# GLA chunks in pairs with five state buffers, the last activation chunk written into the ring, and norms ahead of low parts in the first FFN step

## The chip, the core and the metric

One core of a Trainium2 chip runs the whole program; the metric is the device time of that core in microseconds. TensorE (PE) multiplies into eight PSUM banks of 2 KB per partition, VectorE (DVE), ScalarE (ACT) and GpSimd (POOL) do the elementwise work, and the queues of SyncE (SP), ACT and POOL start the transfers between DRAM and SBUF.

## The reference

One decoder layer in float32 over 512 prompt tokens and 8 x 4 decode tokens, D = 2048:

```python
h = rmsnorm(x, g_mix) * (1 + sc1) + sh1
z = h @ w_in                      # attention, pooling and gated linear attention (GLA) columns
# GLA, per head: chunks of 32 tokens, state S of 128 x 256
def step(S, xs):
    qd_i, kdec_i, v_i, bl_i = xs
    o_i = qd_i @ S                              # what earlier chunks give
    S = exp(bl_i) * S + kdec_i.T @ v_i          # the state after this chunk
    return S, o_i
x = x + g1 * (mix @ w_out)
h2 = rmsnorm(x, g_ffn) * (1 + sc2) + sh2
gate, up = split(h2 @ w_gu)                     # DFF = 5632
x = x + g2 * ((silu(gate) * up) @ w_down)
y = rmsnorm(x, g_final)
```

## The kernel before, in words

Activations lie transposed, 128 features by 544 tokens a tile, in two halves of 272. Every large product is made of three float32r matmuls: high part of the weight by high and by low part of the activation, and low by high. ACT makes the high part of a weight tile (`hi`, `hi_op`), DVE the low part (`lo`, `lo_op`); both run a fixed list of steps, in program order, and so do PE and the queues. Semaphores are the only order between engines.

**GLA.** Each of 4 heads has six projections (gq, gk, gv0, gv1, gg0, gg1). `project` goes over 16 k; after each k it has 6 matmuls (L1887) behind it and runs whatever side jobs are listed for that k. In gg0 from k = 5 and on into gg1 up to k = 4 the side job is one chunk a k: `chunk(c)` multiplies the chunk's keys by its values (L2113, 32 rows of the array, into PSUM bank 2 or 3), for every fourth chunk the masked inner part of a block of 128 tokens (L2116), and then, once the state before this chunk is there, query by state (L2120, 32 columns of the array) into the chunk's 32 partitions of the block's output. Those are plain float32 products, two instructions each in the trace. DVE's `update(c)` (L1424 and L1429) makes the next state from the bank; there are two state buffers, so that states and queries follow each other chunk by chunk. From k = 6 of gg1 on come the eight decode sequences (L2133, L2140). `spread` and `beside` write the lists.

**FFN.** 44 steps make 128 activation features each (gate and up), then 3 x 8 steps multiply by w_down. The first two steps are plain (`plain_product`, eight products of 24 matmuls); from step 2 on a step is seven products (`product`, L2242) over quarters and their combinations, 24 matmuls each, or 18 where a down step spans three chunks. Weights come two steps ahead (`load_group`, SP). An activation chunk is four steps; after steps 4c+3 and 4c+4 (FT = 44 is the first down step) `turn_parts` on DVE and `parts_hi` on ACT make seven quarters with high and low parts in SQ, from where SP (`store_parts`) stores them to DRAM, twice 952 KB. The down steps read a ring of four chunks in HS; POOL fills it from DRAM (`load_parts`, 544 KB for a quarter of a chunk), the first three chunks as the last gate step, FT - 1, sets the place of each quarter free, the fourth right behind them. PE waits for a quarter in `product`. The saved residual comes back by `load_x1` on the same queue.

**Between them.** `last_two` makes the last two tiles of the output projection, first half of the tokens for both tiles, then the second half. `sum_half(w)` adds up the squares for the norm of one half. Then each (half, row half) goes through `norm` (DVE), `affine` (ACT, and POOL for decode columns), `hs_hi` (ACT) and `hs_lo` (DVE), and `plain_product(0, j)` waits for `hs_lo` at j = 0, 2, 4, 6.

Of the kernel before, what the change touches and what calls it, by code (L numbers as in the profile page):

```python
# [32 lines left out]
P = 128  # L33
# [13 lines left out]
GG0_CHUNKS = 11  # L47
# [164 lines left out]

def nth(s, i=0):

    return OPS * (s - PLAIN) + i


def rows_of(s):

    if s < FT:  # L220
        return [V_FFN + V_CHUNK * (s // FC) + 4 * (s % FC) + j for j in range(4)]
    return [V_FFN + V_CHUNK * (v % NFC) + 4 * FC + (s - FT) % DOWN for v in range(*chunks(s))]
# [12 lines left out]
def program(nc, ctx, ins, outs):  # L235
# [98 lines left out]
    SS = [sb(f"SS{i}", [P, DV]) for i in range(2)]  # L334
    SD = sb("SD", [P, DEC_B, DV])
# [48 lines left out]
    TT = sb("TT", [P, 4, HT])  # L384
    SQ = sb("SQ", [P, 2, 7, HT], F32R)
# [40 lines left out]
    def o_block(b):  # L426

        return PS[:, b // 2, DV * (b % 2):DV * (b % 2) + DV]

# [97 lines left out]
    def af_tile(f):  # L527
        return AF[min(f % 4, 2)]
# [7 lines left out]
    def _(sp):  # L536
# [82 lines left out]
    def _(g):  # L619
# [109 lines left out]
        for h in range(GH):  # L729
            if h:  # L730
                g.dma_start(HP[:, :], ins["head_params"][h]).then_inc(S["head_in"], 16)
            g.dma_start(SD[:, :, :], ins["gla_state"][h]).then_inc(S["state_in"], 16)
            g.wait_ge(S["state_up"], NCH * (h + 1))
            g.wait_ge(S["seq_up"], DEC_B * (h + 1))
            g.dma_start(outs["gla_prompt"][h], SS[0][:, :]).then_inc(S["s_out"], 16)
# [79 lines left out]
    def _(a):  # L815
# [290 lines left out]
        def parts_hi(p, n):  # L1106

            if n == 0:
# [3 lines left out]
                a.activation(SQ[:, 0, 0, :], AF[p % 2][:, 0:HT], ACT.Copy).then_inc(S["af_hi"], 1)  # L1112
            elif n == 1:
                a.activation(SQ[:, 0, 1:3, :], halves(AF[2][:, :]), ACT.Copy).then_inc(S["af_hi"], 1)
            else:
                a.wait_ge(S["t_made"], 4 * p + 4)
                a.activation(SQ[:, 0, 3:7, :], TT[:, :, :], ACT.Copy).then_inc(S["af_hi"], 1)
# [61 lines left out]
        rms(1)  # L1179
# [16 lines left out]
        for s in range(PLAIN, STEPS):  # L1196
            u = s - (STEPS - DOWN)
            for i in range(7):
                if s == PLAIN and i == 1:
                    a.wait_ge(S["hs_lo"], 16)  # L1200
                    a.wait_ge(S["taken"], 2)
                    a.activation(AF[0][:, :], AFX[:, :], ACT.Copy)
                if s == PLAIN and i == 2:
                    plain_gates(1, SG[0][:, :], SG[1][:, :])
                slot(s, i)
                if 3 <= s <= FT and s % 4 in (0, 3):
                    p = 2 * ((s - 3) // 4) + (s - 3) % 4
                    if i == 2:
                        parts_hi(p, 0)
                        parts_hi(p, 1)  # L1210
                    elif i == 3:
                        parts_hi(p, 2)
                if (u, i) in SQUARED:
                    square_x1(SQUARED[u, i])
# [13 lines left out]
    def _(d):  # L1228
# [187 lines left out]
        for h in range(GH):  # L1416
# [3 lines left out]
            def update(c):  # L1420
                last = pcol(c, CH) + CH - 1
                d.wait_ge(S["chunk_mm"], NCH * h + c + 1)
                if c == 0:
                    d.tensor_copy(SS[1][:, :], PS[:, 2, 0:DV]).then_inc(S["state_up"], 1)  # L1424
                    return
                if c == 1:
                    d.wait_ge(S["head_in"], 16 * (h + 1))
                d.wait_ge(S["state_up"], NCH * h + c)
                d.scalar_tensor_tensor(out=SS[(c + 1) % 2][:, :], in0=SS[c % 2][:, :], scalar=EB[:, last:last + 1],  # L1429
                                       in1=PS[:, 2 + c % 2, 0:DV], op0=ALU.mult, op1=ALU.add)\  # L1430
# [84 lines left out]
            for c in range(GG0_CHUNKS, NCH):  # L1515
                update(c)
# [134 lines left out]
        def slot(s, i):  # L1651
# [18 lines left out]
            elif i == 6:  # L1670
# [6 lines left out]
                if s < FT:  # L1677
                    d.wait_ge(S["gate_b"], s + 1)
                    d.tensor_tensor(af_tile(s)[:, HT:NT], SG[1][:, :], W5[:, :], ALU.mult).then_inc(S["taken"], 1)
# [9 lines left out]
        def turn_parts(p, n):  # L1689

            b11, b12 = (AF[p % 2][:, HT * a:HT * a + HT] for a in range(2))
            b21, b22 = (AF[2][:, HT * a:HT * a + HT] for a in range(2))
# [10 lines left out]
            elif n == 2:  # L1703
                for x, src, lo_q, up_q in ((1, AF[p % 2][:, 0:HT].unsqueeze(1), 0, 1), (2, halves(AF[2][:, :]), 1, 3)):
                    d.wait_ge(S["af_hi"], 3 * p + x)
                    d.tensor_tensor(SQ[:, 1, lo_q:up_q, :], src, SQ[:, 0, lo_q:up_q, :].bitcast(F32), ALU.subtract)\
                        .then_inc(S["af_lo"], 1)
            else:
                d.wait_ge(S["af_hi"], 3 * p + 3)
                d.tensor_tensor(SQ[:, 1, 3:7, :], TT[:, :, :], SQ[:, 0, 3:7, :].bitcast(F32), ALU.subtract)\  # L1710
                    .then_inc(S["af_lo"], 1)

# [78 lines left out]
        for s in range(PLAIN, STEPS):  # L1791
            for i in range(7):
# [4 lines left out]
                if 3 <= s <= FT and s % 4 in (0, 3) and 1 <= i <= 4:  # L1797
                    turn_parts(2 * ((s - 3) // 4) + (s - 3) % 4, i - 1)
# [15 lines left out]
    def _(e):  # L1814
# [238 lines left out]
        for h in range(GH):  # L2053
# [50 lines left out]
            def chunk(c):  # L2104
                b, rows = c // 4, slice(CH * (c % 4), CH * (c % 4) + CH)
                if c == 0:
                    e.wait_ge(S["gv_by_token"], 4 * h + 4)
                    e.wait_ge(S["a_masked"], 2 * h + 2)
                elif c == 1:
                    pass  # L2110
                else:
                    e.wait_ge(S["state_up"], NCH * h + c - 1)
                e.matmul(PS[:, 2 + c % 2, 0:DV], KDT[rows, b, :], GVT[rows, b, :], start=True, stop=True)\  # L2113
                    .then_inc(S["chunk_mm"], 1)
                if c % 4 == 0:
                    e.matmul(o_block(b), ATT[:, b, :], GVT[:, b, :], start=True, stop=False, skip_group_check=True)  # L2116
                if c:
                    e.wait_ge(S["state_up"], NCH * h + c)
                    at = pcol(c, CH)
                    mm = e.matmul(o_block(b)[rows, :], GQ[:, at:at + CH], SS[c % 2][:, :],  # L2120
                                  start=False, stop=True, skip_group_check=True)
                if c == NCH - 1:
# [32 lines left out]
            beside("gg0", 4, 10, {3: [lambda: v_turn(1)]}, spread(5, chunk, range(GG0_CHUNKS)))  # L2155
            beside("gg1", 5, 10, spread(0, chunk, range(GG0_CHUNKS, NCH)), spread(6, sequence, range(DEC_B)))

# [13 lines left out]
        def last_two():  # L2171
# [4 lines left out]
            for w in range(2):  # L2176
                for t in range(2):
                    for k in range(KT):
# [3 lines left out]
                        if w == 1 and t == 0 and k == 8:  # L2182
# [12 lines left out]
        def plain_product(s, j):  # L2195
# [6 lines left out]
            for k in range(KT // 2):  # L2202
                if s == 0 and j == 1 and k == 4:
# [15 lines left out]
        def product(s, i):  # L2219
# [13 lines left out]
            if s == FT or s > FT and last > chunks(s - 1)[1]:  # L2233
                e.wait_ge(quarter_in[i], 16 * last)
# [210 lines left out]
```

## Time and profile before

| | us |
|---|---|
| median of 3 runs (2534.06 to 2538.4) | 2534.31 |
| the profiled execution | 2530.13 |
| its span, first to last instruction | 2528.3 |
| PE busy | 2400.5 |
| DVE busy | 1549.9 |
| ACT busy | 921.5 |
| transfers, mean over the span | 170 GB/s |

The first three lines are times of the whole program; the others are within the span. Busy time of PE is not time at its peak: matmuls overlap, and an array that drains between two of them is still counted busy.

### The profile page before, as it was taken

The page shows a single profiled execution, that of the slowest core. Times are in us where ns is not written, and L with a number is a line of the kernel's source. Part 1 is how long each engine was busy: PE and PEld are TensorE (multiplying, and loading weights), DVE is VectorE, ACT ScalarE, POOL GpSimd, SP SyncE. Part 2 cuts the span into 40 slices and gives each one's busy share as a digit, 9 for nine tenths or more (in the row PEclk, how much of TensorE's full clock was granted, in tenths as well). Part 3 has the DMA queues.
Part 4 walks back from the last instruction along what each step waited for, and adds up shares of the span by engine and source line. Part 5 has one row for each costly group of instructions (what it writes and reads, how often), then busy time and mean ns, then how long its engine had stood idle before and what let it go on. Part 6 is the DMA issues. An engine that isn't in the chain of part 4 may idle for free.

```text
span 2528.3 us, 44152 instructions
## 1 busy us (share of the span) xinstructions
PE 2400.5 (95%) x18537; PEld 2198.0 (87%) x18537; DVE 1549.9 (61%) x2234; ACT 921.5 (36%) x1322; POOL 238.0 (9%) x292
## 2 busy tenths in 40 slices
PE   5689999999999899989999999999999979999996
PEld 1189887777777599989999999999999979999996
DVE  0332642323223322379888888888888868888898
ACT  2132431313122312354444444444444433433343
POOL 3150230000000011100000000000000121011131
PEclk9889999999999999999999999999999989999998
DMA  9954464545454243223344334433443596366452
GB/s 343 338 181 160 151 185 137 188 150 188 149 174 157 73 156 107 101 101 123 131 168 164 122 131 170 162 122 131 169 162 124 205 399 249 126 226 216 161 209 96
DMA packets 195606, 430.21 MB, mean 170 GB/s; under 512 B 14740, under 2 KB 120516, under 8 KB 193360
## 3 DMA queue, kind: packets, MB, share of 16 engines
q1 hardware_dynamic: 174720, 345.25, 39.8%
q0 software_dynamic: 18096, 77.68, 8.7%
q10 hardware_dynamic: 2592, 4.46, 0.5%
q8 instruction: 147, 2.41, 0.4%
q14 instruction: 51, 0.42, 0.0%
HBM read 369.35 MB, written 57.98 MB: 169 GB/s over the span
## 4 chain that ended last, share of the span: by engine, by line
PE 89%; DMA 4%; DVE 3%; issue 1%; ACT 1%; SPq 0%; POOL 0%; DVEq 0%; ACTq 0%; POOLq 0%
PE PJ L2242 26%; PE PS L2242 26%; PE PJ L1887 24%; DMA AR<-in_weights 3%; PE PJ L1840 2%; PE PS L2113 2%; PE PS L2120 1%; DMA GR<-in_weights 1%; PE PJ L1830 1%; PE PJ L2209 1%; PE PS L2140 1%; PE PS L2133 1%; PE PJ L1852 1%; PE PJ L2186 1%; ACT X L1127 1%
## 5 line engine op out<-in xcount | busy, mean ns | idle before, releaser
L2242 PE MATMUL PS<-HS,WO 128*128 128x272 f32 x5376 | 683.5, 289 | 15.8 <-DVE W L1616 13.7
L2242 PEld LDWEIGHTS PS<-HS,WO 128*128 128x128 f32 x5376 | 679.0, 188 | 16.9 <-DVE W L1616 13.9
L2242 PE MATMUL PJ<-HS,WO 128*128 128x272 f32 x5376 | 681.1, 288 | 0.4 <-DVE WO L1593 0.3
L2242 PEld LDWEIGHTS PJ<-HS,WO 128*128 128x128 f32 x5376 | 677.3, 188 | 0.9 <-issue 0.9
L1081 ACT ACTIVATE WO<-GR 128x1024 fp32r<-128x1024 f32 (+1 forms) x462 | 477.0, 1033 | 495.2 <-PE PJ L2242 233.6
L1593 DVE TENSOR_TENSOR WO<-GR,WO 128x1024 fp32r<-128x1024 f32 (+1 forms) x462 | 556.1, 1204 | 134.4 <-ACT WO L1081 134.3
L1887 PE MATMUL PJ<-HH,WH 128*128 128x272 f32 x1568 | 350.8, 305 | 20.7 <-issue 7.9
L1887 PE MATMUL PJ<-HH,WL 128*128 128x272 f32 x1568 | 327.8, 291 | 0.0
L1887 PE MATMUL PJ<-HL,WH 128*128 128x272 f32 x1568 | 327.7, 291 | 0.0
L1887 PEld LDWEIGHTS PJ<-HH,WH 128*128 128x128 f32 x1568 | 248.0, 192 | 72.4 <-issue 61.3
L1232 DVE TENSOR_TENSOR WL<-RW,WH 128x1024 fp32r<-128x1024 f32 x102 | 128.5, 1264 | 289.7 <-ACT WH L820 289.4
L1887 PEld LDWEIGHTS PJ<-HL,WH 128*128 128x128 f32 x1568 | 250.4, 192 | 0.0
L1887 PEld LDWEIGHTS PJ<-HH,WL 128*128 128x128 f32 x1568 | 249.2, 192 | 0.0
L820 ACT ACTIVATE WH<-RW 128x1024 fp32r<-128x1024 f32 x102 | 107.3, 1054 | 187.1 <-PE PJ L1887 187.1
L1830 PE MATMUL PJ<-AR,CS 128*32 128x512 f32 x256 | 68.7, 685 | 50.4 <-DMA AR<-in_weights 50.2
L775 POOL DMA_DIRECT2D HS<-act_parts x98 | 69.8, 713 | 331.3 <-PE PJ L2242 204.8
L1830 PEld LDWEIGHTS PJ<-AR,CS 128*32 128x32 f32 x256 | 9.8, 115 | 103.2 <-DMA AR<-in_weights 87.5
L1429 DVE SCALAR_TENSOR_TENSOR SS<-SS,EB,PS 128x256 f32<-128x256 f32 x60 | 28.8, 480 | 95.9 <-PE PS L2113 95.9
L780 POOL DMA_DIRECT2D X<-x_kept x4 | 2.3, 566 | 900.2 <-PE PJ L2242 881.2
L1609 DVE TENSOR_TENSOR GR<-GR 128x1024 f32<-128x1024 f32 (+1 forms) x66 | 78.7, 1193 | 6.9
L1616 DVE TENSOR_TENSOR W<-W,PJ 128x272 f32<-128x272 f32 x132 | 57.4, 435 | 36.2 <-PE PJ L2242 35.9
L1601 DVE TENSOR_TENSOR GR<-GR 128x1024 f32<-128x1024 f32 (+1 forms) x66 | 78.3, 1186 | 1.2 <-DMA GR<-in_weights 1.2
(303 smaller groups left out, 1930.5 us busy)
## 6 DMA issues: line engine op xcount, KB each, us to landing
GR<-in_weights SPq DMA_DIRECT2D x264, 512.0 KB, 6.8
AR<-in_weights SPq DMA_DIRECT2D x256, 256.0 KB, 4.6
HS<-act_parts POOLq DMA_DIRECT2D x98, 544.0 KB, 7.0
RW<-in_weights SPq DMA_DIRECT2D x102, 512.0 KB, 4.5
act_parts<-SQ SPq DMA_DIRECT2D x44, 952.0 KB, 7.4
AR<-in_weights SPq DMA_DIRECT2D x64, 512.0 KB, 5.2
MIX<-in_xT SPq DMA_DIRECT2D x1, 4352.0 KB, 16.5
X<-in_xT POOLq DMA_DIRECT2D x4, 1088.0 KB, 9.7
```

What stands on the lines that cost most here:

```text
L775: g.dma_start(HS[:, HS_AT[QUARTER[i]], :, at:at + 2, :].bitcast(F32), XQ[QUARTER[i], :, :, c:c + 2, :])\
L820: a.activation(WH[v.mod(HIS)][:, :], RW[v.mod(RAW)][:, :], ACT.Copy).then_inc(S["hi"], 1)
L1081: a.activation(split_part(n, 0), operand(n), ACT.Copy).then_inc(S["w_hi"], 1)
L1232: d.tensor_tensor(WL[v.mod(RAW)][:, 0:n], RW[v.mod(RAW)][:, 0:n], WH[v.mod(HIS)][:, 0:n].bitcast(F32), ALU.subtract).then_inc(S["lo"], 1)
L1593: d.tensor_tensor(split_part(n, 1), operand(n), split_part(n, 0).bitcast(F32), ALU.subtract)\
L1601: d.tensor_tensor(a21, a21, a22, ALU.add).then_inc(S["combined"], 1)
L1609: d.tensor_tensor(a12, a12, a11, ALU.subtract).then_inc(S["combined"], 1)
L1616: d.tensor_tensor(out[:, :], dst[:, :], src, ALU.add).then_inc(S["sums"], 1)
L1830: mm = e.matmul(PJ[j:j + CP, 2 * pair, :], CS[:, k, :], AR[n % AS][:, 512 * c:512 * c + 512], start=(k < 4), stop=(k >= KT - 4))
L1840: mm = e.matmul(PJ[CP * x:CP * x + CP, 2 * pair, 0:HB], CS[:, 4 * s + x, :], AR[n % AS][:, HB * x:HB * x + HB], start=(s == 0), stop=(s == ...
L1887: mm = e.matmul(out[w], x, y[:, k, HT * w:HT * w + HT], start=(k == 0 and n == 0), stop=(k == KT - 1 and n == 2))
L2242: mm = e.matmul(out, w[part], HS[:, HS_AT[QUARTER[i]], y, (2 * first + k) % (KT // 2), :], start=OPENS[i] and k == 0 and x == 0, stop=k == ...
```

## The change

GLA: five state buffers. `pair_up(n)` issues the key-by-value products of chunks 2n and 2n+1 one behind the other, every second k, and `block_out(b)` the three or four query-by-state products of a block together, two steps later. The other state buffers lie where GB and GT are dead. FFN: the two half chunks of the last activation chunk (p = 20 and 21) are not stored and loaded, but written by ACT and DVE straight into the ring's fourth place, during steps FT and FT+1; the order of chunks in the ring becomes 0, 1, 2, 10, 3, ... First FFN step: on DVE and ACT `norm`, `half_residual`, `reciprocal`, `affine` and `rms` change places with `hs_lo` and `plain_lo`, and PE has `sum_half` earlier.

```diff
+RING = (0, 1, 2, NFC - 1) + tuple(range(3, NFC - 1))
+    TURNED.update({(ss, n + 1): (pp, n) for n in range(4)})
+    PARTED.update({(ss, 2): (pp, (0, 1)), (ss, 3): (pp, (2,))})
+TURNED.update({(FT - 1, 1): (KEPT, 0), (FT - 1, 2): (KEPT, 1), (FT, 1): (KEPT, 2), (FT, 2): (KEPT, 3)})
+TURNED.update({(FT, 3): (KEPT + 1, 0), (FT, 4): (KEPT + 1, 1), (FT + 1, 1): (KEPT + 1, 2), (FT + 1, 2): (KEPT + 1, 3)})
+for pp in range(2):
+    PARTED.update({(FT + pp, 0): (KEPT + pp, (0, 1)), (FT + pp, 1): (KEPT + pp, (2,))})
...
-            if 3 <= s <= FT and s % 4 in (0, 3):
+            if 3 <= s <= FT - 4 and s % 4 in (0, 3):
                 store_parts((s - 3) // 4, (s - 3) % 4)
...
-            if i == 5:
-                g.wait_ge(S["af_lo"], 3 * (2 * NFC - 1))
-                load_x1(1)
-        for i in range(OPS):
-            load_parts(FT - 1, i, 3)
-        g.wait_ge(S["parts_out"], 64 * NFC)
+        g.wait_ge(S["af_lo"], parts_made(KEPT, 4))
+        load_x1(1)
+        for v in range(4, 11):
             for i in range(OPS):
                 load_parts(last_use(v - 4), i, v)
+                if v == 4 and i == 4:
+                    g.wait_ge(S["af_lo"], parts_made(KEPT + 1, 4))
+                    load_x1(2)
+            if v == 4:
+                load_x1(3)
...
+                if p >= KEPT:
+                    a.wait_ge(S["w_used"], nth(FT))
+                    a.activation(HS[:, HS_AT[0], 0, at, :], x[:, 0:HT], ACT.Copy).then_inc(S["af_hi"], 1)
+                    return
...
         affine(0)
         hs_hi(0)
         half_x1(KT - 2, 1)
+        half_x1(KT - 1, 1)
         affine(1)
-        half_x1(KT - 1, 1)
+        rms(1)
         plain_hi(0, 2)
         plain_hi(0, 3)
         hs_hi(1)
-        rms(1)
...
-            for c in range(GG0_CHUNKS):
-                if c == 6:
+            for c in range(12):
+                if c == 4:
                     lo(v + (1 + LEAD))
-                if c == 7:
+                if c == 8:
                     head_mod("gg0")
                 update(c)
...
         norm(0)
+        d.wait_ge(S["x1_out_a"], 32)
+        norm(1)
         half_residual(KT - 2, 1)
         hs_lo(0)
-        d.wait_ge(S["x1_out_a"], 32)
-        norm(1)
         half_residual(KT - 1, 1)
+        reciprocal(1)
         plain_lo(0, 2)
         plain_lo(0, 3)
+        norm(2)
         hs_lo(1)
-        reciprocal(1)
-        norm(2)
-        hs_lo(2)
         d.wait_ge(S["x1_out_b"], 32)
         norm(3)
+        hs_lo(2)
...
+            def pair_up(n):
+                b = n // 2
+                if n == 0:
...
+                else:
+                    e.wait_ge(S["state_up"], NCH * h + 2 * n)
+                for c in (2 * n, 2 * n + 1):
+                    rows = slice(CH * (c % 4), CH * (c % 4) + CH)
+                    e.matmul(chunk_up(c), KDT[rows, b, :], GVT[rows, b, :], start=True, stop=True)\
+                        .then_inc(S["chunk_mm"], 1)
+                if n % 2 == 0:
+                    e.matmul(o_block(b), ATT[:, b, :], GVT[:, b, :], start=True, stop=False, skip_group_check=True)
...
+            def block_out(b):
+                e.wait_ge(S["state_up"], NCH * h + 4 * b + 3)
+                for j in range(4):
+                    c, rows = 4 * b + j, slice(CH * j, CH * j + CH)
+                    if c:
+                        at = pcol(c, CH)
+                        mm = e.matmul(o_block(b)[rows, :], GQ[:, at:at + CH], SS[c % STATES][:, :],
+                                      start=False, stop=True, skip_group_check=True)
...
+                return {k: [lambda: block_out(n // 2 - 1)] + jobs if n and n % 2 == 0 else jobs}
+            beside("gg0", 4, 10, {3: [lambda: v_turn(1)]}, *[chunks_of(5 + 2 * n, n) for n in range(6)])
+            beside("gg1", 5, 10, chunks_of(1, 6), chunks_of(3, 7), {5: [lambda: block_out(NB - 1)]},
+                   spread(6, sequence, range(DEC_B)))
...
-                        if w == 1 and t == 0 and k == 8:
+                        if w == 1 and t == 0 and k == 4:
                             sum_half(0)
...
-                if s == 0 and j == 1 and k == 4:
+                if s == 0 and j == 0 and k == 4:
                     sum_half(1)
...
-                e.wait_ge(quarter_in[i], 16 * last)
+                e.wait_ge(quarter_in[i], 16 * (last - (last > 3)))
+            if s > FT and last == 4 and i == 0:
+                e.wait_ge(S["af_lo"], parts_made(KEPT + 1, 4))
```

## Rows read from the trace of the kernel before

**Rows 1.** The page, chain that ended last: share of the span by engine.

```profile
PE 89%; DMA 4%; DVE 3%; issue 1%; ACT 1%; SPq 0%; POOL 0%; DVEq 0%; ACTq 0%; POOLq 0%
```

**Rows 2.** Chain of work on PE, GLA chunks of head 0: start us, us, what.

```profile
405.15 0.62 PE PS L2113 x2
405.77 0.63 PE PS L2116 x2
406.40 0.76 PE PJ L1887 x6
...
407.78 0.55 PE PS L2120 x2
408.33 0.95 PE PJ L1887 x6
...
440.36 0.95 PE PJ L1887 x6
```

**Rows 3.** The same view, two other lines that use part of the array.

```profile
272.75 1.16 PE PS L1997 x16
...
441.31 1.86 PE PJ L1840 x32
```

**Rows 4.** Timeline of DVE, a state update: start, us, line, operation, [idle <-releaser].

```profile
407.82 0.48 DVE L1429 SCALAR_TENSOR_TENSOR SS<-SS,EB,PS 128x256 f32<-128x256 f32 x1 [1.59 <-PE PS L2113]
```

**Rows 5.** The page, costliest groups: low part of a weight tile, mean ns.

```profile
L1232 DVE TENSOR_TENSOR WL<-RW,WH 128x1024 fp32r<-128x1024 f32 x102 | 128.5, 1264 | 289.7 <-ACT WH L820 289.4
```

**Rows 6.** Timeline of PE, steps FT and FT+1.

```profile
2023.99 9.20 PE L2242 MATMUL PS<-HS,WO 128*128 128x272 f32 x72
2034.41 2.49 PE L2242 MATMUL PS<-HS,WO 128*128 128x272 f32 x18 [1.22 <-issue]
2050.56 6.18 PE L2242 MATMUL PS<-HS,WO 128*128 128x272 f32 x36 [13.66 <-DVE W L1616]
...
2073.41 15.96 PE L2242 MATMUL PS<-HS,WO 128*128 128x272 f32 x126
```

**Rows 7.** Waits, 1990 to 2130 us: who, for whom, us, times, longest.

```profile
ACT SQ L1112 <- DMA act_parts<-SQ: 16.6, 1, 16.6
```

**Rows 8.** Timeline of POOL: loads of the ring's fourth place, held by the third's landing.

```profile
2034.61 0.72 POOL L775 DMA_DIRECT2D HS<-act_parts x1 [3.73 <-DMA HS<-act_parts]
...
2045.84 0.72 POOL L775 DMA_DIRECT2D HS<-act_parts x1 [5.12 <-DMA HS<-act_parts]
```

**Rows 9.** Timeline of SP's queue: stores of the last two half chunks.

```profile
2018.75 1.04 SPq L598 DMA_DIRECT2D act_parts<-SQ  x2
...
2052.61 0.98 SPq L598 DMA_DIRECT2D act_parts<-SQ  x2
```

**Rows 10.** Windows: us, busy of PE PEld DVE ACT POOL, clock, DMA share, GB/s.

```profile
2040.00:2045.00 5.00, 0.00 (x0) 0.00 (x0) 0.00 (x0) 0.00 (x0) 0.71 (x1) 0.50 1.03 414
...
2075.00:2080.00 5.00, 5.00 (x42) 5.00 (x41) 4.90 (x8) 2.38 (x4) 0.39 (x1) 1.00 1.03 414
```

**Rows 11.** Timeline of DVE: low parts of an activation's turned quarters.

```profile
2051.29 1.29 DVE L1710 TENSOR_TENSOR SQ<-TT,SQ 128x1088 fp32r<-128x1088 f32 x1
```

**Rows 12.** Timeline of PE, the first FFN step (j = 0, j = 4) and the second's start.

```profile
1074.46 3.27 PE L2209 MATMUL PS<-HS,WO 128*128 128x272 f32 x24 [1.33 <-DVE HS L1729]
...
1096.41 5.48 PE L2209 MATMUL PS<-HS,WO 128*128 128x272 f32 x24 [4.34 <-DVE HS L1729]
...
1112.44 3.19 PE L2209 MATMUL PJ<-HS,WO 128*128 128x272 f32 x24
```

**Rows 13.** Timeline of DVE there: reciprocal and norm.

```profile
1086.78 1.85 DVE L1723 RECIPROCAL RN<-RN 128x272 f32<-128x272 f32 x1
1088.66 2.50 DVE L1718 TENSOR_TENSOR X<-X,RN 128x1088 f32<-128x1088 f32 x2
```

**Rows 14.** Timeline of ACT there: affine, high parts.

```profile
1067.94 4.05 ACT L1127 ACTIVATE X<-X,MOD 128x256 f32<-128x256 f32 x8 [3.31 <-DVE X L1718]
...
1093.94 2.09 ACT L1139 ACTIVATE HS<-X 128x1088 fp32r<-128x1088 f32 x2
```

More of the change, by code:

```diff
@@ L46 @@
 NCH = SEQ // CH
-GG0_CHUNKS = 11
+STATES = 5
 TAU = 16.0
@@ L210, with parts_made @@
 SQUARED.update({(u, i): 2 * u - (i == 2) for u in range(4, DOWN) for i in (2, 6)})
+KEPT = 2 * NFC - 2
+RING = (0, 1, 2, NFC - 1) + tuple(range(3, NFC - 1))
+TURNED, PARTED = {}, {}
+for pp in range(KEPT):
+    ss = 4 * (pp // 2) + 3 + pp % 2
+    TURNED.update({(ss, n + 1): (pp, n) for n in range(4)})
[4 more added lines that the diff above has]
+    PARTED.update({(FT + pp, 0): (KEPT + pp, (0, 1)), (FT + pp, 1): (KEPT + pp, (2,))})
+def parts_made(p, n):
+    return 3 * p + max(p - KEPT, 0) + n
 def nth(s, i=0):
@@ L221, in rows_of @@
         return [V_FFN + V_CHUNK * (s // FC) + 4 * (s % FC) + j for j in range(4)]
-    return [V_FFN + V_CHUNK * (v % NFC) + 4 * FC + (s - FT) % DOWN for v in range(*chunks(s))]
+    return [V_FFN + V_CHUNK * (v % NFC) + 4 * FC + (s - FT) % DOWN for v in map(lambda v: RING[v % NFC], range(*chunks(s)))]
 def groups_in(s):
@@ L334, in program @@
     SS = [sb(f"SS{i}", [P, DV]) for i in range(2)]
+    SS += [sb(f"SS{i + 2}", [P, DV], at=gb_at + 4 * DV * i) for i in range(STATES - 2)]
     SD = sb("SD", [P, DEC_B, DV])
@@ L428, in o_block, with chunk_up @@
         return PS[:, b // 2, DV * (b % 2):DV * (b % 2) + DV]
+    def chunk_up(c):
+        return PS[:, 2 + c % 2, 0:DV]
     def bank_decode(ps):
@@ L527, in af_tile @@
     def af_tile(f):
-        return AF[min(f % 4, 2)]
+        return AF[3 if f == FT - 1 else min(f % 4, 2)]
     block = ctx.enter_context(nc.Block())
@@ L1106, in parts_hi @@
         def parts_hi(p, n):
+            x, up = AF[p % 2], AF[3 if p > KEPT else 2]
+            at = KT // 2 - 2 + p % 2
             if n == 0:
                 a.wait_ge(S["taken"], 2 * (4 * (p // 2) + p % 2 + 3))
+                if p >= KEPT:
+                    a.wait_ge(S["w_used"], nth(FT))
+                    a.activation(HS[:, HS_AT[0], 0, at, :], x[:, 0:HT], ACT.Copy).then_inc(S["af_hi"], 1)
+                    return
                 if p:
                     a.wait_ge(S["parts_out"], 32 * p)
-                a.activation(SQ[:, 0, 0, :], AF[p % 2][:, 0:HT], ACT.Copy).then_inc(S["af_hi"], 1)
+                a.activation(SQ[:, 0, 0, :], x[:, 0:HT], ACT.Copy).then_inc(S["af_hi"], 1)
             elif n == 1:
-                a.activation(SQ[:, 0, 1:3, :], halves(AF[2][:, :]), ACT.Copy).then_inc(S["af_hi"], 1)
+                out = HS[:, HS_AT[1]:HS_AT[1] + 2, 0, at, :] if p >= KEPT else SQ[:, 0, 1:3, :]
+                a.activation(out, halves(up[:, :]), ACT.Copy).then_inc(S["af_hi"], 1)
             else:
                 a.wait_ge(S["t_made"], 4 * p + 4)
-                a.activation(SQ[:, 0, 3:7, :], TT[:, :, :], ACT.Copy).then_inc(S["af_hi"], 1)
+                if p < KEPT:
+                    a.activation(SQ[:, 0, 3:7, :], TT[:, :, :], ACT.Copy).then_inc(S["af_hi"], 1)
+                    return
+                for y in (0, 2):
+                    q = HS_AT[3 + y]
+                    a.activation(HS[:, q:q + 2, 0, at, :], TT[:, y:y + 2, :], ACT.Copy).then_inc(S["af_hi"], 1)
         def affine(b):
@@ L1205, in _ @@
                 slot(s, i)
[L1206 to L1212, printed above, removed]
+                if (s, i) in PARTED:
+                    for n in PARTED[s, i][1]:
+                        parts_hi(PARTED[s, i][0], n)
                 if (u, i) in SQUARED:
@@ L1514, in _ @@
             lo(v + LEAD)
-            for c in range(GG0_CHUNKS, NCH):
+            for c in range(12, NCH):
                 update(c)
@@ L1691, in turn_parts @@
             b11, b12 = (AF[p % 2][:, HT * a:HT * a + HT] for a in range(2))
-            b21, b22 = (AF[2][:, HT * a:HT * a + HT] for a in range(2))
+            up, at = AF[3 if p > KEPT else 2], KT // 2 - 2 + p % 2
+            b21, b22 = (up[:, HT * a:HT * a + HT] for a in range(2))
             t1, t2, t3, t4 = (TT[:, x, :] for x in range(4))
@@ L1703, in turn_parts @@
             elif n == 2:
[L1704 to L1708, printed above, removed]
+                for x, src, lo_q, up_q in ((1, AF[p % 2][:, 0:HT].unsqueeze(1), 0, 1), (2, halves(up[:, :]), 1, 3)):
+                    q = HS_AT[lo_q]
+                    hi, lo = (HS[:, q:q + up_q - lo_q, part, at, :] if p >= KEPT else SQ[:, part, lo_q:up_q, :]
+                              for part in range(2))
+                    d.wait_ge(S["af_hi"], parts_made(p, x))
+                    d.tensor_tensor(lo, src, hi.bitcast(F32), ALU.subtract).then_inc(S["af_lo"], 1)
+            elif p < KEPT:
                 d.wait_ge(S["af_hi"], 3 * p + 3)
@@ L2154, in _, with chunks_of @@
             beside("gv1", 6, 11, {4: [lambda: v_turn(0)]})
-            beside("gg0", 4, 10, {3: [lambda: v_turn(1)]}, spread(5, chunk, range(GG0_CHUNKS)))
-            beside("gg1", 5, 10, spread(0, chunk, range(GG0_CHUNKS, NCH)), spread(6, sequence, range(DEC_B)))
+            def chunks_of(k, n):
+                jobs = [lambda: pair_up(n)]
+                return {k: [lambda: block_out(n // 2 - 1)] + jobs if n and n % 2 == 0 else jobs}
+            beside("gg0", 4, 10, {3: [lambda: v_turn(1)]}, *[chunks_of(5 + 2 * n, n) for n in range(6)])
+            beside("gg1", 5, 10, chunks_of(1, 6), chunks_of(3, 7), {5: [lambda: block_out(NB - 1)]},
+                   spread(6, sequence, range(DEC_B)))
         project_two(At(M_OUT), At(T_OUT), KT, A_FIRST + N_HB, {4: [lambda: o_turn(GH - 1)]})
@@ L2232, in product @@
             first, last = chunks(s)
-            if s == FT or s > FT and last > chunks(s - 1)[1]:
-                e.wait_ge(quarter_in[i], 16 * last)
+            if s == FT or s > FT and last > chunks(s - 1)[1] and last > 4:
+                e.wait_ge(quarter_in[i], 16 * (last - (last > 3)))
+            if s > FT and last == 4 and i == 0:
+                e.wait_ge(S["af_lo"], parts_made(KEPT + 1, 4))
             n, tiles = nth(s, i), 2 * slots(s)
```

51 lines of the change are left out of this document (19 added, 32 removed).

## The prediction

> **What bounds the kernel now.** I read the page first. The chain that ended last is PE for 89% of the span [rows 1], so a change pays by what it takes off PE: products, drains of the array, waits. Then I read the chain of work on PE and the timelines of the three places that the diff touches.
>
> *GLA chunks.* Six projection matmuls (L1887) take 0.76 us when they follow a full-array product and 0.95 us when they follow a chunk's query product [rows 2]. So leaving a part-array product for the full array costs 0.19 us. A chunk adds 0.62 (L2113) and 0.55 (L2120), and every fourth 0.63 more (L2116). There is no wait on a semaphore that matters here: PE is the bound, with work that fills little of the array. From the first chunk (405.15) to the matmuls behind the last (440.36) are 35.21 us; 15 groups at 0.76 and 0.4 for turning modulation rows leave 23.4. From below: 16 x 0.62 + 4 x 0.63 + 15 x 0.55 = 20.7, and 14 returns to the full array at 0.19 = 2.7, together 23.4. The other three heads repeat the pattern.
>
> *First down steps.* 126 matmuls take 15.8 us (the last row of [rows 6] shows 15.96 with the end of the last one). FT starts at 2023.99, FT+2 at 2073.41, where 31.6 us would do: 17.8 us are lost. PE stands 13.66 us for a sum on DVE. DVE was behind ACT, and ACT waited 16.6 us for a store of SQ [rows 7] which was issued at 2018.75 [rows 9], when the transfers were saturated: about 414 GB/s at a DMA share of 1.03 [rows 10]. In the same stretch PE's clock fell to 0.50 of full, its lower level of 1.2 GHz. Quarters 4 and 6 of the first three ring chunks had landed at 2034.6 and 2045.8, since the fourth chunk's loads wait for that [rows 8].
>
> *First FFN step.* Its eight products of 24 matmuls and one sum (1.25 us) would take 25.4 us without waits. They begin at 1074.46, 1.33 us late, and the second step begins at 1112.44 [rows 12]: 39.3 from 1073.1, so 14 us are lost. The longest wait, 4.34 us, brought the lower clock: 24 matmuls in 5.48 instead of 3.2. All these waits end with `hs_lo` or with the squares of the second half.
>
> **Part 1, GLA in pairs.** What decides is whether products on different strips of the array overlap. The trace has both kinds. L1840 puts 16 products (32 instructions of 256 columns) on four column strips in turn: 1.86 us [rows 3]. By L2113, one such instruction costs (0.62 - 0.19)/2 = 0.215, so one behind the other they would take 6.9; 1.86 is 8 x 0.215 and a drain. Column strips overlap fully. L1997 alternates between two row strips into two banks: 16 instructions of 128 columns in 1.16 [rows 3], against 16 x 0.107 + 0.19 = 1.9 in series and 1.05 if perfectly overlapped, so row strips overlap too, at some 10% over the ideal. Hence a `block_out` costs 2 x 0.215 + 0.16, 0.6 us, and a `pair_up` 0.19 + 0.43 x 1.1 = 0.66.
>
> A head then has 8 x 0.66 + 4 x 0.63 + 4 x 0.6 = 10.2, and four odd pairs that go straight back to the full array at 0.2, together 11.0. The last `block_out` goes into L1840, which uses the same strips. Before it was 23.4 and one return more: 23.6. Saved: 12.5 a head, 50 us for four. The upper bound, with ideal overlap, is 52. The lower, with every product in series, is 0.43 more a pair and 1.29 (once 0.86) more a block: 11.0 + 3.4 + 4.7 = 19.1 a head, 18 us saved in all. I take 50, since both kinds of overlap have a row.
>
> The Trainium skill, "TensorE: Matmul & The Clock Gate", Part 3, says that a weight load runs ahead of matmuls in flight only when its row strip differs. The four products of `block_out` share all rows, so by that rule they go one after another, and part 1 saves about 19 us less; L1840's 32 instructions in 1.86 us speak against it. The same skill, "TensorEngine Tiling (Array Packing)", Key Properties, says that a change of tiling mode drains the array; by that rule, the trace agrees: 0.95 against 0.76.
>
> The added wait: `pair_up(n)` needs both banks, so `update(2n-1)`. An update starts 0.73 us after its L2113 and takes 0.48 [rows 2, 4]; two dependent ones are done some 1.9 us after the pair's start. The next pair comes after 0.66, 0.2 and 12 matmuls (1.51), 2.4 us: 0.4 us of slack. Queued behind that wait is everything on PE. The low part of a weight tile (1.26 us, [rows 5]) now stands between updates 3 and 4 on DVE. Its high part on ACT starts when k = 7 is done, together with pair 1, and takes 1.06, so DVE is free 3.1 us after pair 1's start; update 4's products end at 3.7. It is covered; without that cover it would cost 1.3 us a head. The first tile of gg1 is alike. DVE's and ACT's other work, and the weight loads, have longer leads.
>
> **Part 2, last activation chunk into the ring.** Gone are four stores of 952 KB (two before 2046, two after), seven ring loads of 544 KB, ACT's wait for SQ, and SP's wait for p = 21 ahead of the weights of FT+2. At 2019.8 some 6.4 MB of ring loads and 1.5 MB of weights are left; at 0.41 MB/us these take 19.3 us, so quarter 6 lands at about 2039 instead of 2045.8, and PE wants it at 2037.6: about 1 us. No long idle, so the clock stays at 2.4 GHz.
>
> What is late next is DVE. A down step over three chunks keeps it busy 4.90 of 5 us at PE's pace [rows 10]. FT now also has the low parts of p = 20 (1.07 and 1.29 [rows 11]) and four subtractions for p = 21 (1.7), FT+1 the low parts of p = 21 (2.4). Walking down DVE's list with 0.95 a weight part, 0.44 a sum and 0.75 a residual, the low weight parts come late by 0.5 at FT+1's first product, 1.2 at its third and 0.7 at its sixth. With the quarter's 1 us that overlaps them, FT+2 starts at about 2058.3 instead of 2073.4: 15 us saved. ACT's copies (0.42 to 0.65 each) fit into its idle half. POOL's queue: tile 3 of the residual now comes behind quarter 6, wanted 15 us later; tiles 4 to 7 are issued at about 2054 behind two ring loads and wanted by DVE at 2065; at half the bandwidth they land at 2061. Bounds: 17.8 if nothing is late, and about 5 if the quarters land as before.
>
> **Part 3, norms first.** I walk the three lists with reciprocal 1.85, a norm 2.5 and low parts of the same size [rows 13], affine 4.05 and high parts 2.09 [rows 14]. `sum_half(0)` comes 1.5 us earlier, so `hs_lo(0)` is ready at 1072.6 and PE goes on without the first wait. The squares of the second half are ready at 1074.9, and the sum waits 0.5. But then DVE stands at `reciprocal(1)`, now in front of `plain_lo(0, 2)`, `plain_lo(0, 3)`, `norm(2)` and `hs_lo(1)`: ACT gives `rms(1)` only behind `affine(1)`, at 1079.4. 1.85 + 2.4 + 2.5 + 1.2 later, at 1087.4, comes `hs_lo(1)`, which PE wants at 1080.8: a new wait of 6.7 us at j = 2, with 2.3 us for the lower clock as before [rows 12]. From there on nothing is late: `norm(3)`, `hs_lo(2)` and `hs_lo(3)` are ready at 1092.3 and 1098.6, PE wants them at 1096 and 1102. Loss 9.5 instead of 14: 4.5 us saved; bounds 0 and 7.5.
>
> **Sum.** 50 + 15 + 4.5 = 69.5 us. The profiled execution took 2530.1, so 2460.6; the median shown is 4.2 above it, so 2464.8 in the runs.
>
> **The rivals.**
> - *A, strips do not overlap.* For: nothing here packs this pair of shapes. Against: [rows 3]. Column strips alone in series: 19 us less, 2484. Both in series: 32 less, 2497.
> - *B, the junction stays bound by transfers.* The stretch is saturated from 2009 to 2090 us, and weights of FT+1 now share it earlier with the ring loads. If quarter 6 lands at 2045.8 still, PE waits 8 us and runs slow for a while: part 2 gives 5, the time is 2475.
> - *C, slower.* DVE's two updates do not fit between two pairs, PE stands before every pair, and the granted clock falls to half through gg0 and gg1. A head's window of some 23 us then doubles: 4 x 23 = 92 lost against 69.5 won, 2557. It decides from gaps like the 4.34 us one [rows 12]; gaps of 1.3 us left the clock alone, and the slack above is positive. Unlikely.
> - *D, the new order of norms gives nothing or a loss* (`reciprocal(1)` waits longer than I have it): 4.5 to 8 less, 2469 to 2473.
>
> **How the numbers follow.** Forecast with its own range 2458 to 2472: 0.66 (D lies within or just beside it, 0.07); B 0.13; A with column strips alone 0.06, both 0.04; C 0.02; the rest 0.02. The range of 8 in 10, 2457 to 2480, takes in B and leaves out A and C. This kernel can be told from no change by about 0.2%, 5 us. Only C is slower: faster 0.97, same 0.01, slower 0.02.
>
> **What would show it.** L2113 as four instructions in 0.66 us and L2120 as eight in 0.6; 12.5 us a head less from first chunk to first decode sequence; more than 1 us each, or a wait of PE for L1429's successor, refutes part 1. From FT to FT+2 33 to 35 us with no wait for a store, and only short waits for low weight parts; a wait of PE near 8 us in FT is B. In the first FFN step one long wait at its third product and none at its fifth and seventh, second step starting 39.3 - 4.5 = 35 us after the output projection's end. The forecast fails if the gain of GLA is under 40 us or if a wait appears that the trace of before does not have in GLA.

## The result, and the profile after

Times are medians in us, each beside the kernel before on the same chip. Ratios have 95% intervals.

| | before | changed | ratio |
|---|---|---|---|
| time | 2535.51 (2534.06 to 2538.4) | 2468.03 (2466.91 to 2471.12) | 0.9737 [0.9721, 0.9752] |
| profiled execution, its span | 2530.13, 2528.3 | 2467.32, 2465.5 | |
| last two tiles of the output projection begin | 1047.37 | 993.75 | |
| second FFN step begins | 1112.44 | 1055.30 | |
| FT begins | 2023.99 | 1966.84 | |
| FT+2 begins | 2073.41 | 2010.64 | |

The change is faster by 67.5 us. The marks divide the 62.8 us between the two profiled executions without a rest: 53.6 before the last two tiles, 3.5 from there to the second FFN step, 5.6 from FT to FT+2, and 454.9 us from FT+2 to the end in both. The 4.7 us that are left of 67.5 lie between profiled and median executions: 5.4 in the kernel before, 0.7 in the changed one.

The page of the changed kernel, its chain by engine, answers to [rows 1]:

```profile
PE 91%; DMA 3%; DVE 2%; issue 2%; ACT 1%; SPq 0%; POOL 0%; DVEq 0%; POOLq 0%; ACTq 0%
```

PE bounds the kernel even more. Its chain in the GLA chunks of head 0 (start us, us, what) answers to [rows 2]. L2150 is `pair_up`, L2153 the masked block, L2161 `block_out`, L1924 the projection and L1877 the ada half:

```profile
404.60 0.63 PE PS L2150 x4
405.23 0.63 PE PS L2153 x2
405.86 1.50 PE PJ L1924 x12
407.36 0.63 PE PS L2150 x4
408.00 1.69 PE PJ L1924 x12
409.68 0.56 PE PS L2161 x6
410.25 0.63 PE PS L2150 x4
...
427.10 0.57 PE PS L2161 x8
427.66 1.73 PE PJ L1877 x32
```

A pair of chunks takes 0.63 where one chunk took 0.62, and four query products take 0.57 where one took 0.55. From the first chunk to the ada half are 23.06 us, before 36.16 (405.15 to 441.31): 13.1 a head. The other three heads have the same two figures, so the four stretches give 52.4 of the 53.6 us; 0.55 more is a first chunk that starts earlier (404.60 for 405.15), and 0.7 lies elsewhere. Nothing on PE waits for an update.

The junction (steps FT and FT+1, where the gate steps give way to the down steps), timeline of PE in the changed kernel, answers to [rows 6]:

```profile
1966.84 6.93 PE L2290 MATMUL PS<-HS,WO 128*128 128x272 f32 x54
1974.80 2.50 PE L2290 MATMUL PS<-HS,WO 128*128 128x272 f32 x18 [1.03 <-issue]
1979.02 2.48 PE L2290 MATMUL PS<-HS,WO 128*128 128x272 f32 x18 [1.72 <-issue]
1983.23 2.49 PE L2290 MATMUL PS<-HS,WO 128*128 128x272 f32 x18 [1.74 <-issue]
1990.78 4.22 PE L2290 MATMUL PS<-HS,WO 128*128 128x272 f32 x18 [5.06 <-issue]
1994.84 15.96 PE L2290 MATMUL PJ<-HS,WO 128*128 128x272 f32 x126
2010.64 15.96 PE L2290 MATMUL PS<-HS,WO 128*128 128x272 f32 x126
```

The wait of 13.66 us for DVE has gone. In its place PE waits ahead of each of the last four products of FT, 9.55 us together, and the trace names no instruction as releaser; what is due there is a quarter of the ring ("issue" is all that the view has for it). The seventh product starts 23.94 us after FT does. The windows (columns as in [rows 10]) show the transfers and the clock there:

```profile
1950.00:1990.00 40.00, 31.24 (x244) 30.45 (x242) 30.42 (x52) 14.50 (x22) 15.07 (x22) 0.97 0.98 377
...
1990.00:1995.00 5.00, 4.22 (x20) 4.25 (x21) 0.00 (x0) 0.00 (x0) 0.00 (x0) 0.54 0.05 16
```

The transfers are saturated for 40 us, and nearly empty once the quarter is there. That this wait is one for transfers is shown by e4_group_late and e9_half_loads below. The clock is then at 0.54 of full, near its lower level of 1.2 GHz, so that 18 matmuls take 4.22 instead of 2.5.

The first FFN step, timeline of PE in the changed kernel, answers to [rows 12]:

```profile
1019.58 1.75 PE L2255 MATMUL PS<-HS,WO 128*128 128x272 f32 x12
1021.80 0.70 PE L2214 MATMUL PJ<-AC,CN 128*128 128x272 f32 x2 [0.47 <-ACT QX L1074]
...
1034.06 5.40 PE L2255 MATMUL PS<-HS,WY 128*128 128x272 f32 x24 [6.11 <-DVE HS L1766]
...
1049.17 3.29 PE L2255 MATMUL PS<-HS,WY 128*128 128x272 f32 x24 [0.65 <-DVE HS L1766]
...
1055.30 3.19 PE L2255 MATMUL PJ<-HS,WO 128*128 128x272 f32 x24
```

The first wait is gone, and one wait of 6.11 us stands ahead of the third product, with the lower clock behind it (0.54 of full from 1034.06 to 1039.30). `hs_lo(1)` is late because of what DVE does ahead of it, and that begins with a wait for ACT's `rms(1)`. Timeline of DVE:

```profile
1026.06 1.85 DVE L1760 RECIPROCAL RN<-RN 128x272 f32<-128x272 f32 x1 [4.87 <-ACT RN L1185]
...
1030.23 2.49 DVE L1755 TENSOR_TENSOR X<-X,RN 128x1088 f32<-128x1088 f32 x2
```

### The profile page after: what moved, and what is told of

Its sections match the earlier page's. It is cut to its first block, busy times and chain, and to the rows that moved or that the text cites. A ratio compares the mean times of both kernels' runs of the same rounds, so it can differ in the third digit from the quotient of the medians.

```text
span 2465.5 us, 44142 instructions
## 1 busy us (share of the span) xinstructions
PE 2346.9 (95%) x18537; PEld 2182.4 (89%) x18537; DVE 1553.5 (63%) x2236; ACT 921.7 (37%) x1324; POOL 238.7 (10%) x285
## 4 chain that ended last, share of the span: by engine, by line
PE 91%; DMA 3%; DVE 2%; issue 2%; ACT 1%; SPq 0%; POOL 0%; DVEq 0%; POOLq 0%; ACTq 0%
PE PJ L2290 27%; PE PS L2290 27%; PE PJ L1924 25%; DMA AR<-in_weights 3%; PE PJ L1877 2%; PE PJ L1867 1%; PE PJ L2255 1%; PE PS L2150 1%; PE PS L2181 1%; PE PS L2255 1%; PE PS L2174 1%; PE PJ L1889 1%; PE PJ L2232 1%; DVE X L1844 0%; PE PS L2153 0%
## 5 line engine op out<-in xcount | busy, mean ns | idle before, releaser
L1924 PE MATMUL PJ<-HH,WH 128*128 128x272 f32 x1568 | 348.1, 304 | 20.7 <-issue 7.9
L1924 PE MATMUL PJ<-HL,WH 128*128 128x272 f32 x1568 | 327.7, 291 | 0.0
L1924 PE MATMUL PJ<-HH,WL 128*128 128x272 f32 x1568 | 327.5, 291 | 0.0
L1924 PEld LDWEIGHTS PJ<-HH,WH 128*128 128x128 f32 x1568 | 248.7, 191 | 55.2 <-issue 43.3
L1924 PEld LDWEIGHTS PJ<-HL,WH 128*128 128x128 f32 x1568 | 250.0, 191 | 0.0
L1924 PEld LDWEIGHTS PJ<-HH,WL 128*128 128x128 f32 x1568 | 249.4, 192 | 0.0
L798 POOL DMA_DIRECT2D HS<-act_parts x91 | 64.8, 713 | 343.0 <-PE PJ L2290 231.7
L1642 DVE TENSOR_TENSOR W<-W,PS 128x272 f32<-128x272 f32 x132 | 57.3, 434 | 41.7 <-PE PS L2290 41.3
```

What stands on the lines that cost most here:

```text
L1642: d.tensor_tensor(out[:, :], dst[:, :], src, ALU.add).then_inc(S["sums"], 1)
L1924: mm = e.matmul(out[w], x, y[:, k, HT * w:HT * w + HT], start=(k == 0 and n == 0), stop=(k == KT - 1 and n == 2))
```

## The experiments

| kernel | median | ratio | last two tiles to second FFN step | FT to FT+2 |
|---|---|---|---|---|
| before | 2535.5 | 1 | 65.1 | 49.42 |
| changed | 2468.03 | 0.9737 [0.9721, 0.9752] | 61.55 | 43.80 |
| e1_gla | 2479.41 | 0.9772 [0.9752, 0.9791] | 66.5 | 49.30 |
| e2_ring | 2529.44 | 0.9976 [0.9964, 0.9987] | 66.5 | 44.96 |
| e3_norms | 2528.16 | 0.9968 [0.9956, 0.998] | 61.6 | 49.18 |
| e4_group_late | 2465.43 | 0.9719 [0.9703, 0.9735] | 61.0 | 39.14 |
| e5_outs_single (one run) | 2499.93 | | 61.7 | |
| e6_chunks_single (one run) | 2495.83 | | 61.6 | |
| e7_rms_early | 2463.71 | 0.9724 [0.9707, 0.974] | 56.3 | 44.2 |
| e8_both | 2459.63 | 0.9708 [0.9693, 0.9722] | 54.8 | 38.8 |
| e9_half_loads (one run) | 2466.82 | | 61.2 | 33.34 |
| r1_changed | 2470.03 | 0.9753 [0.9739, 0.9766] | 61.2 | 43.7 |
| r2_both | 2457.45 | 0.9704 [0.969, 0.9717] | 54.8 | 38.7 |

The work before the last two tiles differs from run to run: in the kernels with the new GLA code and the same instructions up to there, these tiles began at 993.7 to 1003.9. So what a local edit does is read from its own stretch in the trace first, and from the median second.

### One part alone: e1_gla, e2_ring, e3_norms

Each is the kernel before with the hunks of one part; the core of each:

```diff
 e1_gla:   beside("gg0", ...)
-  spread(5, chunk, range(GG0_CHUNKS))
+  *[chunks_of(5 + 2 * n, n) for n in range(6)]
 e2_ring:  SP
-  if 3 <= s <= FT and s % 4 in (0, 3):
+  if 3 <= s <= FT - 4 and s % 4 in (0, 3):
 e3_norms: DVE
   norm(0)
+  d.wait_ge(S["x1_out_a"], 32)
+  norm(1)
   half_residual(KT - 2, 1)
   hs_lo(0)
...
```

> The kernel before with the GLA part of the change alone (pairs, blocks, five state buffers). The changed kernel reached its output projection's last two tiles 53.6 us earlier than the kernel before. Theory 'parts add up': this kernel starts them as early, and its time is 53 to 54 us under the kernel before, about 2482. Rival 'part of the GLA gain came out of weights and lists that the other parts touch', which would leave less than 50 us here.

> The kernel before with the ring part alone (last activation chunk straight into the ring, chunk order changed). The forecast's step said 15 us; the changed kernel's trace has 5.6 between FT and FT+2. Theory 'bound by transfers': 5 to 6.5 us under the kernel before, steps FT and FT+1 take 43.5 to 44 us, and PE waits at the fourth to seventh product of FT for ring loads, the seventh some 24 us after FT's start. Rival 'GLA or norms shift something into the junction': here it would be 10 us or more.

> The kernel before with the new order of norms alone. Theory: 3 to 4 us under the kernel before, from the last two tiles' start to the second FFN step 61.5 us instead of 65.1, with one wait of about 6 us at the third product of the first step. Rival: no difference within 1 us, if what the list gains is given back later in the FFN.

Measured: 55.8, 5.7 and 7.0 us, 68.5 together against 67.5 for the whole. Each of the three differences is known to some 3 to 5 us, so the parts add up as far as these runs can tell.

e1_gla was expected to begin the last two tiles 53.6 us earlier; in its trace it is 47.8 (999.6). Its first chunk starts 5.3 us later than before (410.48), and from there on it has the gain of the changed kernel: 23.06 or 23.07 us a head. By its own stretch, part 2 alone saves 4.5 (49.42 to 44.96); FT to FT+2 was expected at 43.5 to 44.

Part 3 alone gave more than the 3 to 4 us expected: its interval is 0.20 to 0.44%, 5 to 11 us. By its own stretch it saves 3.5 (65.1 to 61.6) against the profiled execution of the kernel before. But e1_gla and e2_ring, which keep the old order of norms, have 66.5 there, and the seven traces with the new order and without e7's edit have 61.0 to 61.7. So the part is worth 3.5 to 5 us in its stretch; why the old order gives 65.1 once and 66.5 twice stays open, and so does what of the 7.0 lies beyond. Timeline of PE at the junction of e2_ring:

```profile
2047.00 2.49 PE L2278 MATMUL PS<-HS,WO 128*128 128x272 f32 x18 [1.72 <-issue]
2054.70 4.42 PE L2278 MATMUL PS<-HS,WO 128*128 128x272 f32 x18 [5.22 <-issue]
```

The same wait ahead of the seventh product, which starts 24.3 us after FT, with the old GLA and the old norms: it belongs to the ring part alone.

### The junction: e4_group_late, e9_half_loads

Three groups of transfers share the stretch ahead of that product: the ring's quarters and the weights of FT+1 and FT+2. The last were held behind a store in the kernel before. e4 holds them until the last quarter has landed:

```diff
         for s in range(STEPS):
+            if s == FT:
+                sp.wait_ge(quarter_in[6], 48)
             if s + 2 < STEPS:
                 load_group(s + 2)
```

> The changed kernel, with SP waiting for the seventh quarter of the first three ring chunks before it loads the weights of FT+2 (1.57 MB, in the changed kernel issued before those quarters have landed, since SP no longer waits there for the last store). Theory 'these weights take the ring loads' share': the quarter lands about 4 us earlier (20 instead of 23.9 us after FT's start), PE's last wait in FT shrinks from 5.1 to 1 or 2 us and the clock stays up, so 4 to 6 us under the changed kernel, about 2463. Rival 'the ring loads have a limit of their own, 0.3 MB/us, whatever else runs': no change, or 1 us longer for late weights.

Timeline of PE in e4_group_late:

```profile
1969.73 6.93 PE L2292 MATMUL PS<-HS,WO 128*128 128x272 f32 x54
1978.15 2.50 PE L2292 MATMUL PS<-HS,WO 128*128 128x272 f32 x18 [1.48 <-issue]
1982.36 2.49 PE L2292 MATMUL PS<-HS,WO 128*128 128x272 f32 x18 [1.70 <-issue]
1986.58 2.49 PE L2292 MATMUL PS<-HS,WO 128*128 128x272 f32 x18 [1.72 <-issue]
1990.72 2.50 PE L2292 MATMUL PS<-HS,WO 128*128 128x272 f32 x18 [1.66 <-DVE W L1644]
...
2008.87 3.42 PE L2292 MATMUL PS<-HS,WO 128*128 128x272 f32 x26
```

The seventh product starts 20.99 us after FT, 2.95 sooner, its 18 matmuls stay at 2.5, and FT+2 starts 39.14 after FT instead of 43.80: 4.7 us. The weights of FT+2 were thus one cause of two. The last line names a sum on DVE as releaser, but all of these sums are done by 1990.08; SP, which waits for the landing of the same quarter, issues its held weights at 1990.65, and PE starts at 1990.72. So it is the quarter that PE waits for. The products now follow one another every 4.2 us (a quarter of three chunks is 1.67 MB, 0.40 MB/us), where 2.5 would do: transfers are still the bound. The medians of e4 and the changed kernel differ by 2.6 us, where 4 to 6 were expected, and their intervals overlap; the price of 4.7 is read from the stretch. e8_both and e7_rms_early, two kernels that differ in this wait alone, have 38.8 and 44.2 there.

e9 is e4 and leaves out the low parts in the loads of the first three ring chunks, so that they move half the bytes:

```diff
+            parts = slice(0, 1) if v < 3 else slice(0, 2)
-            g.dma_start(HS[:, HS_AT[QUARTER[i]], :, at:at + 2, :]...
+            g.dma_start(HS[:, HS_AT[QUARTER[i]], parts, at:at + 2, :]...
```

> The kernel with the weights of FT+2 held (e4), whose first three ring chunks are loaded with their high parts only, so that the ring loads before FT are half the bytes (the low parts of these chunks, part of the computation, are left out). It asks what would bound FT and FT+1 if transfers did not. Theory of the forecast: DVE then, late by 1.2 to 2.4 us over both steps, so 33 to 34 us from FT to FT+2 instead of 39.1 (31.6 would be without any wait), the first four to seven products of FT without gaps. Rival 'something other than bandwidth holds the quarters' (the issue on POOL, their order): 37 us or more.

Timeline of PE in e9_half_loads:

```profile
1976.63 11.45 PE L2293 MATMUL PS<-HS,WO 128*128 128x272 f32 x90
1988.42 4.80 PE L2293 MATMUL PS<-HS,WO 128*128 128x272 f32 x36 [0.34 <-DVE W L1645]
1993.06 11.83 PE L2293 MATMUL PJ<-HS,WO 128*128 128x272 f32 x90
2005.36 4.78 PE L2293 MATMUL PJ<-HS,WO 128*128 128x272 f32 x36 [0.47 <-DVE W L1645]
2009.97 2.29 PE L2293 MATMUL PS<-HS,WO 128*128 128x272 f32 x17
```

33.34 us from FT to FT+2, with 0.8 us of waits for a sum on DVE, each ahead of the sixth product of its step, and none for a quarter. That is about the junction that the prediction drew (34.3); only its transfers weren't that small. The time of this one run is no better than e4's, since its last two tiles begin 6.7 us later (1003.9 for 997.2).

### What the overlap of strips is worth: e5_outs_single, e6_chunks_single

e5 keeps the pairs, but puts each query product behind its own update, between projection steps. e6 keeps `block_out`, and puts one chunk where a pair was.

```diff
 e5:
-            def block_out(b):
-                e.wait_ge(S["state_up"], NCH * h + 4 * b + 3)
-                for j in range(4):
+            def block_out(b, js):
+                for j in js:
...
+                        e.wait_ge(S["state_up"], NCH * h + c)
...
 e6:
-            def pair_up(n):
+            def single(c):
...
-                for c in (2 * n, 2 * n + 1):
...
```

> The changed kernel with pairs kept, but the query products of a block apart again, one behind each k (k0-3 to k0), so that only row strips can overlap. Theory 'both kinds overlap': a head's stretch from the first chunk to the decode sequences grows from 23.1 us by 15 x 0.55 - 4 x 0.57 = 6.0 for the products and about 1.4 for returns to the full array, to 30 to 31 us, 29 us over four heads. Rival 'column strips do not overlap': then the block of four would already be four times 0.43, and the growth would be only about 3 us a head.

> The changed kernel with blocks kept, but the key-by-value products of each chunk apart again, one chunk behind each k, so that only column strips can overlap. Theory 'both kinds overlap': a head's stretch grows from 23.1 us by 8 x 0.62 = 5.0 for the products and 8 x 0.19 = 1.5 for returns to the full array, to 29.5 us, 26 us over four heads. Rival 'row strips do not overlap, the gain is in fewer returns': growth of 1.5 us a head only.

Chain of work on PE in e5_outs_single, head 0:

```profile
411.02 0.63 PE PS L2150 x4
411.65 0.96 PE PJ L1924 x6
412.61 0.55 PE PS L2161 x2
413.16 0.95 PE PJ L1924 x6
```

A query product costs 0.55 alone and 0.57 in fours, and six projection matmuls take 0.95 behind it instead of 0.75. The head's stretch is 30.45 us (407.71 to 438.16) against 23.06: 7.4 more. e6 has 29.61 (403.84 to 433.45), 6.55 more, with a single chunk at 0.62. The rivals, column strips that don't overlap for e5 and row strips that don't for e6, would have had 3 and 1.5 more. Together 13.95 where the whole part took 13.1 off a head: the two steps account for it. The one run of each is 32.9 and 37.0 us below the kernel before on the same chip, where the changed kernel has 67.5.

### The first FFN step: e7_rms_early

ACT's `rms(1)` and the high parts of two plain weight tiles go ahead of `affine(1)`, the low parts of these tiles ahead of `reciprocal(1)`, and `hs_hi(3)` and `hs_lo(3)` ahead of a part of the next weights:

```diff
 ACT
-        half_x1(KT - 1, 1)
-        affine(1)
-        rms(1)
         plain_hi(0, 2)
+        half_x1(KT - 1, 1)
         plain_hi(0, 3)
+        rms(1)
+        affine(1)
...
+        hs_hi(3)
         plain_hi(1, 0)
-        hs_hi(3)
 DVE
-        reciprocal(1)
         plain_lo(0, 2)
         plain_lo(0, 3)
+        reciprocal(1)
...
+        hs_lo(3)
         plain_lo(1, 0)
-        hs_lo(3)
```

> The changed kernel with the second half's rms ahead of affine(1) on ACT, and the two weight parts made ahead of it in the time in which both engines wait for the last residual. Theory: reciprocal(1) comes at 1077 instead of 1079.5 on the clock of the forecast's walk, hs_lo(1) at 1083.4 instead of 1087.4, so PE's wait at the third product shrinks from 6.1 to 2 to 3 us, the clock stays up and nothing later waits: from the last two tiles' start to the second FFN step 54.5 to 56 us instead of 61.6, 5 to 6 us under the changed kernel. Rival 'the wait moves to hs_lo(2) or hs_lo(3)': 1 to 2 us gained.

Timeline of PE in e7_rms_early:

```profile
1035.86 4.76 PE L2255 MATMUL PS<-HS,WY 128*128 128x272 f32 x24 [2.40 <-DVE HS L1766]
```

The wait falls from 6.11 to 2.40 us, that of the seventh product goes, and the stretch is 56.3 us against 61.55; 54.5 to 56 were expected, and the lower clock makes the difference (last section). So it was what stood in front of `hs_lo(1)`, as the prediction had it. e7 moves `rms(1)` on ACT and the low parts on DVE at once, and doesn't say how much each gave.

### Both: e8_both, r1_changed, r2_both

e8_both and r2_both are e7 with e4's wait; r1_changed is the changed kernel again, on the chip of r2_both.

> The changed kernel with both repairs: weights of FT+2 held until the seventh quarter has landed, and rms early. If the two stretches are independent, 4.7 + 5.5 = 10 us under the changed kernel, about 2458, with steps FT and FT+1 in 39 us. Rival: a shorter first stretch changes nothing in the junction, but the gains are partly lost to waits elsewhere, 2462 or more.

> The changed kernel once more, on the same chip as the next run, so that the two repairs are compared with it directly: 2465 to 2470 us.

> The kernel with both repairs, beside the changed kernel. Theory 'each stretch gives what its trace shows' (4.7 us from FT to FT+2, 6.7 us up to the second FFN step): 10 to 12 us under it. Rival 'traces differ more in their first third than in these stretches, and part is noise': 5 us or less.

2459.63 and 2457.45 us; the second is 12.6 below the changed kernel on the same chip, and the intervals of the ratios, [0.969, 0.9717] and [0.9739, 0.9766], are apart. The two stretches of these two traces give 6.4 (61.2 to 54.8) and 5.0 (43.7 to 38.7), 11.4. It is the fastest version that was run.

## Why the prediction was nearly right

It said 2464.8, and 2468.03 was measured. Its sum was 69.5 us from one profiled execution to the other, where 62.8 came; it put the median 4.2 above the profiled execution, and that was 0.7. The errors of 6.7 and 3.5 go against each other. Within the sum part 2 gave 9.4 less than it had, part 1 3.6 more. So that the time came out within 3.2 us is in part luck: by the prediction's own prices, with what happened at the junction (rival B) it would have been 2475.

*Part 1: right, 52.4 for 50.* Each price held: a pair 0.63 (0.66), a block 0.57 (0.6), a return to the full array 0.19. 13.1 a head came for 12.5, of which these smaller prices give 0.36 (eight pairs and four blocks, 0.03 each); 0.13 more is in L1877, 1.73 for 1.86, behind products on the same strips. Rival A fell: products in series would have made a block 1.7 (4 x 0.43), and the trace has 0.57. The Trainium skill, "TensorE: Matmul & The Clock Gate", Part 3, has a weight load run ahead of matmuls only when its row strip differs; the prediction's reading of it, four products with all rows in common one after another, does not hold here, and the measurement decides. Rival C fell too: DVE ends the two updates 1.7 us after a pair's start (the prediction had 1.9), and the next pair starts 1.0 us or more behind that, for 0.4. Timeline of DVE in the changed kernel, updates of the pair that starts at 407.36:

```profile
408.03 1.06 DVE L1455 SCALAR_TENSOR_TENSOR SS<-SS,EB,PS 128x256 f32<-128x256 f32 x2 [1.74 <-PE PS L2150]
```

*Part 2: mis-sized, 5.6 for 15.* What was to go went: the stores, the wait of ACT and the 13.66 us. The term that failed is the quarter's landing, "quarter 6 lands at about 2039", 15 us after FT. PE started on it after 23.94 us.

The prediction counted from 2019.8, 4.2 us ahead of FT, and had 7.9 MB to move in 19.3 us. From that point to PE's start on the quarter (1962.65 to 1990.78) the changed kernel moves 10.9 MB in 28.1 us, 0.39 MB/us for 0.41. Two amounts were wrong. First, the 6.4 MB of ring loads left at 2019.8: 21 loads of 0.557 MB are 11.7 MB, and 4.3 had moved by then, so 7.4 were left. Second, the weights of FT+2. The prediction counted SP's wait ahead of them as a gain; these 1.57 MB now run beside the ring loads, and e4 shows their price: 2.95 us in the landing, 4.7 by FT+2, since the clock stays up. With 0.28 MB of residual that is 3.0 MB more, 7.3 us at 0.41 MB/us; the lower rate adds 1.5, 8.8 of the 8.9 by which the quarter came late.

The prediction had the clock at 2.4 GHz throughout ("no long idle"); behind the wait of 5.06 us it was 0.54 of full. Low parts and sums on DVE were priced about right: e9, without waits for transfers, takes 33.34 us for the prediction's 34.3. From 1950 to 1990 the changed kernel moves 15.07 MB (377 GB/s for 40 us): 11.7 of ring, two groups of weights at 1.57, 0.28 of residual. In effect and in size that is rival B: it had 5 for part 2. It named the weights of FT+1 as cause, where e4 shows those of FT+2; what FT+1's cost was not tried.

*Part 3: right, 3.5 to 5 for 4.5.* The new wait at the third product is 6.11 (6.7), the one for the squares 0.47 (0.5), the lower clock costs 2.2 (2.3). The cause is the one it gave, `reciprocal(1)` behind ACT's `affine(1)` and `rms(1)`. The prediction had nothing late at the seventh product, which waits 0.65. It was a step that traded one long wait for another; e7 shows that it could have been 5 us more.

*The cover of the median.* The prediction carried the 4.2 us between the profiled execution and the median of before over to the changed kernel. In this kernel that distance is no constant, since the last two tiles begin at 993.7 to 1003.9 in different executions; what makes them differ stays open.

## What to carry to other kernels

Products that use part of the array are worth packing: what costs is the number of changes between part-array and full-array work and the time of one product, not the number of products side by side. When a store or a wait is taken out of a saturated stretch, sum all bytes that can now move ahead of the one transfer that matters, those which the old wait held back among them; a wait that keeps later loads behind an urgent one can be worth keeping. Where a norm's chain is moved forward, look for what now stands between the slowest operation and the tile that PE wants next.

## What the runs showed of the hardware that was not expected

A wait of 2.40 us in front of the same product let the clock fall in e7_rms_early (24 matmuls in 4.76 us, granted clock 0.66 of full from 1035 to 1040) but not in e8_both (1.00 from 1035 to 1040), whose code is the same up to there but for one wait on SP near the end. Timeline of PE in e8_both:

```profile
1035.03 3.26 PE L2257 MATMUL PS<-HS,WY 128*128 128x272 f32 x24 [2.40 <-DVE HS L1768]
```

r2_both has the same wait of 2.40 and 3.26 behind it. So gaps of that length went either way in these runs, and the 1.5 us between the two stretches (56.3 and 54.8) is this alone. Gaps of 1.66 to 1.74 us left the clock alone in all.
